# Delta rule: four independent VectorE steps and a mask move from ahead of the triangular inversion's levels to behind each level's subtractions

## The reference, cut to what matters

```python
G = jnp.cumsum(gc, axis=-1)
L = jnp.exp(jnp.where(incl, G[..., :, None] - G[..., None, :], -jnp.inf))
kb = kc * bc[..., None]
A = jnp.where(strict, jnp.einsum('bnhtd,bnhsd->bnhts', kb, kc) * L, 0.0)
T = lax.linalg.triangular_solve(eye + A, eye, left_side=True, lower=True, unit_diagonal=True)
U = T @ (vc * bc[..., None]);  W = T @ (kb * jnp.exp(G)[..., None])
qk = jnp.where(incl, jnp.einsum('bnhtd,bnhsd->bnhts', qc, kc) * L, 0.0)
q_dec = qc * jnp.exp(G)[..., None]
k_dec = kc * jnp.exp(G[..., -1:] - G)[..., None]
g_last = jnp.exp(G[..., -1])
def step(state, inp):
    u, w, qd, kd, qkc, gl = inp
    v_new = u - w @ state
    o = qd @ state + qkc @ v_new
    state = gl[..., None, None] * state + jnp.swapaxes(kd, -1, -2) @ v_new
    return state, o
```

## Time and profile before

| | us |
|---|---|
| median of 3 runs | 3227.34 |
| lowest and highest of them | 3224.16, 3232.58 |
| the profiled execution's own time | 3227.0 |
| its span | 3225.2 |
| TensorE busy in it | 2927.1 (91%) |
| VectorE busy in it | 1059.7 (33%) |
| ScalarE busy in it | 912.0 (28%) |

### The profile page before, as it was taken

One profiled execution on the slowest core, in us unless ns is written; L12 is line 12 of the kernel. 1 busy time (PEld: TensorE's weight loads), 2 busy tenths in 40 slices (PEclk: granted clock), 3 DMA queues, 4 the chain that ended last, 5 costly groups with the idle time before them and its releaser, 6 DMA issues.

```text
span 3225.2 us, 41374 instructions
## 1 busy us (share of the span) xinstructions
PE 2927.1 (91%) x18323; PEld 2008.5 (62%) x18323; DVE 1059.7 (33%) x1567; ACT 912.0 (28%) x1498; POOL 0.2 (0%) x4
## 2 busy tenths in 40 slices
PE   6997899999998899999989998889998987999897
PEld 3775778888776677888767666644543454544443
DVE  3446642232545743223253334410000135000002
ACT  3444232222444333223243453311100032110011
POOL 0000000000000000000000000000000000000000
PEclk8998999999998899999999999999999998999999
DMA  7224322323223422322372104579999953999997
GB/s 276 79 105 158 106 78 93 94 95 98 69 91 118 159 79 79 104 92 82 109 249 79 40 27 183 195 306 409 409 400 409 404 178 130 404 409 409 402 409 287
DMA packets 251538, 637.26 MB, mean 198 GB/s; under 512 B 12896, under 2 KB 110176, under 8 KB 251232
## 3 DMA queue, kind: packets, MB, share of 16 engines
q1 hardware_dynamic: 248224, 627.22, 52.4%
q10 hardware_dynamic: 3136, 7.40, 0.6%
HBM read 632.48 MB, written 2.10 MB: 197 GB/s over the span
## 4 chain that ended last, share of the span: by engine, by line
PE 70%; DMA 12%; DVE 6%; ACT 5%; PEld 3%; issue 2%; PEldq 1%; SPq 1%; ACTq 0%; DVEq 0%
PE ps L641 68%; DMA ring<-in_w_exp_up 6%; DMA ring<-in_w_exp_gate 5%; PE ps L655 3%; PEld ps L641 3%; ACT h L1657 1%; ACT mix_halves L1660 1%; PEldq L1116 1%; DMA ring<-in_ada_w 1%; SPq L629 0%; DVE work L2398 0%; DVE work L3045 0%; DVE small L2959 0%; DVE work L2961 0%; DVE h L2386 0%
## 5 line engine op out<-in xcount | busy, mean ns | idle before, releaser
L641 PE MATMUL ps<-mix_halves,work_halves 128*128 128x512 f32 (+1 forms) x1544 | 622.4, 403 | 41.6 <-DVE h_halves L2249 33.3
L641 PE MATMUL ps<-h_halves,work_halves 128*128 128x512 f32 (+1 forms) x1544 | 609.4, 395 | 4.8 <-DVE mix_halves L2249 2.4
L641 PE MATMUL ps<-mix_halves,ring_halves 128*128 128x512 f32 x1448 | 569.5, 393 | 0.0
L641 PE MATMUL ps<-ring,work 128*64 128x512 f32 x1552 | 395.7, 595 | 58.9 <-DMA ring<-in_w_exp_up 32.6
L2249 DVE TENSOR_TENSOR ring_halves<-ring,work_halves 128x2048 fp32r<-128x2048 f32 (+2 forms) x125 | 252.6, 2021 | 548.5 <-ACT work_halves L1580 452.9
L641 PEld LDWEIGHTS ps<-mix_halves,work_halves 128*128 128x128 f32 (+1 forms) x1544 | 290.9, 188 | 128.5 <-issue 47.1
L641 PEld LDWEIGHTS ps<-h_halves,work_halves 128*128 128x128 f32 (+1 forms) x1544 | 292.0, 189 | 72.1 <-issue 6.4
L641 PEld LDWEIGHTS ps<-mix_halves,ring_halves 128*128 128x128 f32 x1448 | 273.3, 189 | 60.9
L641 PEld LDWEIGHTS ps<-ring,work 128*64 128x64 f32 x1552 | 129.4, 137 | 272.3 <-issue 270.8
L1580 ACT ACTIVATE work_halves<-ring 128x2048 fp32r<-128x2048 f32 x102 | 188.2, 1845 | 336.7 <-PE ps L641 336.1
L641 PE MATMUL ps<-ring,proj 128*64 128x512 f32 (+1 forms) x1136 | 231.2, 546 | 3.1 <-issue 2.9
(11 more groups left out here) (394 smaller groups left out, 3341.2 us busy)
## 6 DMA issues: line engine op xcount, KB each, us to landing
ring<-in_w_exp_down SPq DMA_DIRECT2D x110, 1024.0 KB, 16.3
ring<-in_w_exp_gate SPq DMA_DIRECT2D x106, 1024.0 KB, 11.4
ring<-in_w_exp_up SPq DMA_DIRECT2D x88, 1024.0 KB, 15.3
ring<-in_ada_w SPq DMA_DIRECT2D x48, 1024.0 KB, 7.4
ring<-in_w_mod SPq DMA_DIRECT2D x48, 1024.0 KB, 7.9
ring<-in_w_in SPq DMA_DIRECT2D x22, 1024.0 KB, 5.3
ring<-in_w_gate SPq DMA_DIRECT2D x22, 1024.0 KB, 5.3
ring<-in_w_up SPq DMA_DIRECT2D x22, 1024.0 KB, 5.4
```

The lines of the kernel that those rows point to most:

```text
L641: i = pe.matmul(o, lhsT, rhs, start=start, stop=stop, **kw)
```

## The change

The five steps are taken out of VectorE's list ahead of the levels. One of each is issued behind the four subtractions of the levels n = 0 to 3, and the mask of the scores behind the wait for the last level's Y, ahead of the copies of Y. TensorE counts `gn` ahead of its first products of level 0 but no longer waits for it; its wait for `mod_ready` stays.

```diff
@@ TensorE, delta(l)
                     if n == 0:
-                        pe.wait_ge(*due("gn"))
+                        due("gn")
                         pe.wait_ge(*due("mod_ready"))
@@ VectorE, delta(l)
                 q = proj[:, 14:16, :]
-                link(tt(g_kb, g_kb, g_eg, ALU.mult))
-                link(tt(q, q, g_eg, ALU.mult))
                 level_blocks(0)
-                link(tt(by16(g_qk), by16(g_qk), const("upto").unsqueeze(1).to_broadcast([P, 16, P]), ALU.mult))
-                link(gated_out(1, 4, param(f"hgrn_norm{l}"), proj[:, 12:14, :], gn_rstd))
                 dve.wait_ge(*due("g_kdf"))
                 dve.wait_ge(*due("g_k_sb"))
-                for c in range(NT):
-                    v = g_kdt[:, c, :].rearrange("p (h e) -> p h e", h=4)
-                    i = tt(v, v, hc(g_kdf)[:, :, c:c + 1].to_broadcast([P, 4, 64]), ALU.mult)
-                link(i)
+
+                def scaled_keys():
+                    for c in range(NT):
+                        v = g_kdt[:, c, :].rearrange("p (h e) -> p h e", h=4)
+                        i = tt(v, v, hc(g_kdf)[:, :, c:c + 1].to_broadcast([P, 4, 64]), ALU.mult)
+                    link(i)
+
+                def masked_scores():
+                    link(tt(by16(g_qk), by16(g_qk), const("upto").unsqueeze(1).to_broadcast([P, 16, P]), ALU.mult))
+
+                def beside(n):
+
+                    if n == 0:
+                        link(tt(g_kb, g_kb, g_eg, ALU.mult))
+                    elif n == 1:
+                        link(tt(q, q, g_eg, ALU.mult))
+                    elif n == 2:
+                        link(gated_out(1, 4, param(f"hgrn_norm{l}"), proj[:, 12:14, :], gn_rstd))
+                    elif n == 3:
+                        scaled_keys()
+                    else:
+                        masked_scores()
+
                 dve.wait_ge(*due("g_t_sb", 2))
                 columns_out(PLANS[f"layer{l}"], 4, 4)
@@
                             dve.wait_ge(*due(name))
                             to(signal, tt(v[:, eight_of(half), :], v[:, eight_of(half), :], change(bank, half), ALU.subtract))
+                    if n < len(LEVELS) - 3:
+                        beside(n)
                 due("g_x", 4)
                 dve.wait_ge(*due("g_yt", 2 * (len(LEVELS) - 2)))
+                beside(len(LEVELS) - 3)
                 dve.tensor_copy(g_Yq[0:64, :, 0, :], g_Yc[0:64, :, :])
```

## The result

| | before | changed |
|---|---|---|
| median of 20 runs each, us | 3226.18 | 3234.07 |
| lowest and highest | 3221.79, 3239.36 | 3222.02, 3244.84 |
| ratio | | 1.0024 (1.0013 to 1.0036) |
| the profiled execution's time, us | 3227.0 | 3227.59 |
| first X of the levels to the first product of chunk 0, layer 1, us | 37.31 | 40.00 |

The forecast was 3223.7, within 3218 to 3230. The median is 0.24% longer, which is clear of noise, and the sign is not the one forecast. The profiled execution of the changed kernel is one of the shortest of its 20: ahead of the stage it is already 2.7 us earlier than the one of before, so the stage has to be read by itself.

A forecast was written before the change was run, and what follows sets the result against it. TensorE was taken as the bound (70% of the chain), held ahead of the levels by VectorE's list. Saving 6.89 us there and paying 3.24 for the mask gave -3.65 us, so 3223.7 us, range 3218 to 3230.

The forecast's parts named there:

- The pause: TensorE's wait ahead of level 0's first products, laid to VectorE's list; closing it saves 3.41 and 3.48 us, 6.89 in all.
- VectorE's steps in the levels cost nothing: Steps queued behind levels 0 to 3 hide under TensorE's products: cost 0, bounds 0 and 2.6 us.
- Rival D: VectorE becomes the bound of the levels; 1.3 us a layer come back, giving 3226.3 us; chance 0.10.
- The mask behind the levels: Mask ahead of the copies delays clearing the state and the first chunk: 1.62 us a layer, 3.24 for two.
- I take no change: TensorE's clock in the chunks taken as unchanged: 0, with bounds of -2.61 and +2.61 us a layer.
- rival B: Longer idleness ahead of the chunks brings a second low-clock stretch, 2.61 us a layer, giving 3228.9 us; chance 0.12.
- Elsewhere: Outside the moved steps: no instruction or transfer added or removed, the weights' four transfers already issued before the pause; no cost counted.
- My sum of -3.65: Forecast total for both layers: -6.89 us from the pause plus 3.24 us for the mask behind the levels.

The follow-up runs named there:

- the series with +18: The changed kernel run and profiled again without any edit: median of 6 runs 3243.61 us, ratio 1.0056 to the kernel before.
- the placement: Changed kernel with decayed keys and queries ahead of `columns_out`, gated block, scaled keys and mask behind levels 0, 1 and 3, transfers at their old time: 1.0004 to before.

## Why the prediction was wrong, step by step

*The pause: right.* Forecast 3.41 and 3.48 us saved, measured 3.36 and 3.44 (groups start 1.94 and 1.93 us after X, against 5.30 and 5.37). The reading of the pause as VectorE's list and `mod_ready` was right too.

*VectorE's steps in the levels cost nothing: right.* With the weights held back, 962 records follow without a stop behind the same VectorE list. Rival D did not happen.

*The mask behind the levels: the direct price was right* (1.62 forecast, 1.54 measured), *the clock's part was not*. "I take no change" of the clock failed. From first product to second chunk's, chunk 0 took 9.00 us before and 9.54 now, and the low clock there lasted 10.24 us in five of the six stages of the changed kernel's three profiles, where it had been 6.83:

```profile
366.00:368.00 2.00, 0.00 (x0) 0.00 (x0) 1.87 (x4) 0.18 (x1) 0.00 (x0) 0.54 0.00 0
368.00:370.00 2.00, 1.25 (x5) 0.99 (x5) 0.62 (x3) 0.00 (x0) 0.00 (x0) 0.50 0.00 0
...
374.00:376.00 2.00, 2.00 (x16) 1.21 (x17) 0.40 (x1) 0.00 (x0) 0.00 (x0) 0.50 0.00 0
376.00:378.00 2.00, 2.00 (x34) 0.98 (x27) 0.64 (x3) 0.00 (x0) 0.00 (x0) 0.90 0.00 0
```

Against the earlier trace rows the low clock now begins in the idle time and lasts longer. That is rival B in kind, at a smaller size (some 0.8 us a layer in the chunks, not 2.61). But the mask is not its only cause. With the mask ahead and the stops left in (two runs), the low clock lasted 10.24 us in the first layer and 6.83 in the second; with the mask behind and no stops (two runs), 6.83 in the first (in one of them a second time before the stage's end) and 10.24 in the second. Only without either was it 6.83 in every stage (eight stages of four profiles).

*The step that failed* is the one under "Elsewhere": that the transfers which run during the pause "were issued before it" and so are of no account. It put their effect on TensorE at nothing, as they had been issued already. They held up TensorE's own instructions, and the pause had hidden that. With TensorE idle, late instructions cost next to nothing; with TensorE at 256 instructions in 3.9 us, each layer lost 5.4 and 4.2 us to them (stretch of 40.00 and 38.78 against 34.59 without). The pause itself was no sign of it: the run of before with the weights held back shows that it was VectorE's list. But the trace of before had such a stop outside the changed place, under transfers at 389 to 419 GB/s, ahead of the last record of a group of 64:

```profile
278.37 1.15 PE L641 MATMUL ps<-h 64*64 64x64 f32 x63 [0.79 <-DVE h L2406]
280.49 0.21 PE L641 MATMUL ps<-h 64*64 64x64 f32 x1 [0.96 <-issue]
```

It is 635 records ahead of the changed kernel's first stop, which is five times 127, and the next record starts 1.5 us after the end of a packet of instructions. The right question was what *else* would be late next besides engines.

The sum over two layers, from the mean of the changed kernel's three profiles: pause -6.8; mask's direct price +3.1; late instructions +9.0 (9.6, 8.1 and 9.3), of which 5.5 are the stops and the rest products at 1.2 GHz behind them and small gaps; first layer's own small gaps, gone, -0.9; chunks at the low clock +1.6. Together +6.0, and the stages measured 131.6 against 125.6. My sum of -3.65 had the first two. The rest of the +7.9 in the medians, 1.9 us, and the further 10 us of the series with +18, is not in this stage. Over all 32 runs of the changed kernel the mean granted clock was 0.9640, over the 83 runs of before in the three later series 0.9664, and within kernels 0.001 goes with 2.3 us. By this estimate the clock goes with 5 to 6 of the 10 us between the means (3236.5 and 3226.6), part of it in this stage; no run sets the clock by itself. What makes it fall more often in stages that were only shifted is not settled.

## What to carry to other kernels

Before closing a pause of an engine that issues many small instructions, look at what the DMA engines do in it. In this program TensorE's instructions came over them too, in a queue of their own, and the pause under heavy traffic was the time in which they arrived. Stops labelled "issue" in the middle of a group, an equal number of instructions apart, are the mark of it, and a packet of the instruction queue that ended 1.2 to 1.5 us before each stop's end confirmed it here. Moving or spreading the bulk transfer is then the edit that makes the other one pay: neither the placement nor the held transfers alone gained anything that could be measured here (1.0004 and 0.9999), together they gave 0.23 to 0.25%. And an elementwise step goes into a stretch where its engine is seen idle; put behind the levels, the mask stood ahead of what the first chunk waits for, and cost 9.6 us in the medians (7.5 in the means) for 3.1 of direct waiting.

## What the runs showed of the hardware

- TensorE stopped for instructions under DMA traffic of 349 GB/s, up to 2.90 us at a time, at places fixed to the instruction's number in the list, 127 or 128 matmul records (with as many weight loads) apart. Copies from DRAM to DRAM did the same as transfers to the on-chip memory.
- All 23 of these stops ended 1.2 to 1.5 us after the end of a 16 KB packet of the instruction queue. With the weights held back the packets for the same blocks ended 2.0 us or more before they were wanted, and there was no such stop.
- Behind a stop of 2.81 us the granted clock went to 0.50, behind the idle time of 3.22 us in the kernel before it did not the earlier trace rows. Idle time alone didn't decide.
- A 64 x 64 matmul in fp32 makes two matmul records and two weight loads.
- The stops cost more than themselves: of 9.0 us lost to late instructions, 5.5 are idle time.
